# Second block's attention: the first head's rough scores and maxima moved into the projections, the last value tiles into the heads, each head's factor spread behind its scores

## The reference, cut to what matters

```
hn = rms_norm_2(x, norm1_g);  proj = hn @ w_in            # 512 tokens, 1024 -> 18 tiles of 128 features
qa, ka, va, qb, kb, vb = split(proj)                      # A: 8 query heads, 2 key/value heads; B: 8 of each
qa, ka = rope(rms_norm_2(qa)), rope(rms_norm_2(ka))       # norm over the 64 features of a head
out_a = softmax(qa ka^T / 8) va                           # all 512 keys
out_b = mixture over three dilated windows of softmax(rms_norm_2(qb) rms_norm_2(kb)^T / 8 + bias) vb
x = x + concat(rms_norm_2(out_a), rms_norm_2(out_b)) @ w_out
```

## Time and profile before

| | |
|---|---|
| median of 3 runs | 2938.24 us (2937.76 to 2941.49) |
| the profiled execution: time, span | 2937.71 us, 2935.9 us |
| TensorE busy | 2868.0 us (98%), granted clock 0.995 on the mean |
| VectorE, ScalarE, GpSimd busy | 1373.8 us, 1140.3 us, 15.2 us |
| last projection tile's products end | about 2366.1 us from the span's start |
| attention block | 2369.4 to 2513.5 us |

### The profile page before, as it was taken

How to read it: one execution, slowest core, us unless ns; L and a number is a source line. 1 busy time by engine, 2 the same in 40 slices (tenths; PEclk the granted TensorE clock), 3 DMA queues, 4 the chain that set the end, 5 groups by cost and what they waited for, 6 DMA issues and landing times. The chain is left out here.

```text
span 2935.9 us, 41186 instructions
## 1 busy us (share of the span) xinstructions
PE 2868.0 (98%) x17312; PEld 2416.9 (82%) x17312; DVE 1373.8 (47%) x1900; ACT 1140.3 (39%) x1633; POOL 15.2 (1%) x28
## 2 busy tenths in 40 slices
PE   7999999999999999999999999999999999999998
PEld 7888888778888888888888878888888878888887
DVE  3334355676333354333346677233354367655641
ACT  3223244544222244232234555222245356444430
POOL 0000000000000000000000000000000000000000
PEclk9999999999999999999999999999999999999999
DMA  4223411103223421223412103223432201222231
GB/s 150 94 101 127 144 35 58 42 3 115 86 100 108 143 101 58 94 93 121 143 37 78 49 3 109 79 93 101 144 103 78 72 27 39 101 66 100 94 129 51
DMA packets 71560, 254.50 MB, mean 87 GB/s; under 512 B 8072, under 2 KB 9224, under 8 KB 71376
## 3 DMA queue, kind: packets, MB, share of 16 engines
q1 hardware_dynamic: 71376, 251.86, 25.5%
HBM read 249.73 MB, written 2.10 MB: 86 GB/s over the span
## 5 line engine op out<-in xcount | busy, mean ns | idle before, releaser
L214 PE MATMUL ps<-h_hi,w_space 128*128 128x512 f32 (+1 forms) x5056 | 1444.5, 369 | 2.9 <-DVE h_lo L312 2.9
L214 PEld LDWEIGHTS ps<-h_hi,w_space 128*128 128x128 f32 x5056 | 918.5, 189 | 164.0 <-DVE h_lo L312 3.6
L202 DVE TENSOR_TENSOR w_space<-w_raw,w_space 128x1024 fp32r<-128x1024 f32 x440 | 533.7, 1224 | 1016.9 <-ACT w_space L195 1016.8
L214 PE MATMUL ps<-h_lo,w_space 128*128 128x512 f32 (+1 forms) x2528 | 929.8, 368 | 0.0
L195 ACT CAST w_space<-w_raw 128x1024 fp32r<-128x1024 f32 x440 | 457.0, 1051 | 899.9 <-PE ps L214 550.2
L224 PE MATMUL ps<-w_space 128*128 128x512 f32 x3216 | 739.9, 391 | 2.3 <-PEq L91 1.4
L224 PEld LDWEIGHTS ps<-w_space 128*128 128x128 f32 x3216 | 604.2, 188 | 127.9 <-issue 1.6
L214 PEld LDWEIGHTS ps<-h_lo,w_space 128*128 128x128 f32 x2528 | 477.5, 189 | 77.5 <-issue 0.5
L589 ACT CAST w_space<-act_p 128x512 fp32r<-128x512 f32 x88 | 54.8, 623 | 186.1 <-DVE act_p L601 186.1
L604 DVE TENSOR_TENSOR w_space<-act_p,w_space 128x512 fp32r<-128x512 f32 x88 | 61.0, 693 | 60.6 <-ACT w_space L589 60.6
L601 DVE TENSOR_TENSOR act_p<-act_s,ps 128x512 f32<-128x512 f32 x88 | 60.0, 682 | 54.9 <-PE ps L214 54.9
(11 more groups left out here) (407 smaller groups left out, 2227.2 us busy)
## 6 DMA issues: line engine op xcount, KB each, us to landing
w_raw<-in_w_ffn_in SPq DMA_DIRECT2D x176, 512.0 KB, 3.5
w_raw<-in_w_ffn_out SPq DMA_DIRECT2D x88, 512.0 KB, 3.6
w_raw<-in_w_in SPq DMA_DIRECT2D x64, 512.0 KB, 3.5
w_raw<-in_w_up SPq DMA_DIRECT2D x44, 512.0 KB, 3.5
w_raw<-in_w_out SPq DMA_DIRECT2D x24, 512.0 KB, 4.1
w_raw<-in_w_down SPq DMA_DIRECT2D x22, 512.0 KB, 3.5
w_raw<-in_w_ple_gate SPq DMA_DIRECT2D x16, 512.0 KB, 3.6
gain_pre<-in_gains_pre SPq DMA_DIRECT2D x10, 512.0 KB, 4.7
```

The lines of the kernel that those rows point to most:

```text
L202: nc.vector.tensor_tensor(self.lo(n), self.raw[:, n % SLOTS, :], self.hi(n).bitcast(F32), ALU.subtract).then_inc(self.lo_ready, 1)
L214: m = nc.tensor.matmul(c.ps[:, bank, t], part[:, cols], moving[:, k, t], start=(k == 0 and i == 0), stop=(k == KD - 1 and i == 2))
```

## The change

- Behind tile 16 TensorE also makes the first head's four rough scores, in banks 2, 3, 6 and 7, and turns two value tiles (banks 5 and 4) instead of one; behind tile 17 and at the end no value tile is turned, only the maxima.
- VectorE takes those four maxima and negates them behind tile 16, and writes the rows of maxima behind tile 17. ScalarE makes `first_k_hi` for head 0 behind tile 14, runs one Exp on one column behind the roots of tile 16, and copies two value tiles there; its copies at the end go.
- GpSimd writes the ones rows of `first_k_hi`. One of two subtractions for `first_q` goes.
- Attention starts with head 0's scores; head 1's rough scores are dealt among them, the exponents of head 0 come ahead of the second head's operands.
- In heads 0 to 7 the spread comes behind the scores. Value tiles 3 and 4 (of five) are turned at the end of heads 2 and 4 (bank 7), and ScalarE copies them there behind that head's exponents.

```diff
+def write_top_rows(nc, c, rows, bank):      # as top_rows before
+def values_to_tokens(nc, c, bank, tile):    # four transposes, as values_back before
+def copy_token_values(nc, c, bank, j):      # as copy_values before
...
-    SUM_BANK, SPREAD_BANKS, VALUE_BANKS = 4, (2, 3), (5, 2, 3, 6, 7)
+    SUM_BANK, SPREAD_BANKS, VALUE_BANKS = 4, (2, 3), (5, 5, 4)
+    ROUGH_BANKS, TOP_BANK = (2, 3, 6, 7), 7
...
     def tensor_after(self, pe, nc, n):
...
-        if n >= 16:
-            if n == 16:
-                pe.wait_ge(self.normed, self.NA)
-            self.values_back(pe, nc, n - 15)
+        if n == 16:
+            pe.wait_ge(self.normed, self.NA)
+            pe.wait_ge(self.first_lo, 2)
+            for i, bank in enumerate(self.ROUGH_BANKS):
+                nc.tensor.matmul(c.ps[:, bank, :], c.first_q[:, 0, i * P:(i + 1) * P], c.first_k[:, :], start=True,
+                                 stop=True).then_inc(self.rough, 1)
+            pe.wait_ge(self.v_copied, 1)
+            self.values_back(pe, nc, 1)
+            pe.wait_ge(self.rooted, 2)
+            self.values_back(pe, nc, 2)
 
     def tensor_end(self, pe, nc):
-        self.values_back(pe, nc, 3)
-        self.values_back(pe, nc, 4)
+        pe.wait_ge(self.tops_low, 1)
+        nc.tensor.transpose(self.c.ps[0:NT, self.TOP_BANK, S - P:S], self.neg_top[:, :],
+                            self.c.mat["ident"]).then_inc(self.tops_turned, 1)
...
         if n == 16:
             self.roots(act, nc, self.NA, len(self.TILES))
-        if n == 17:
+            nc.scalar.activation(self.unread[:, :], c.eps[:, 0:1], ACT.Exp)
             self.copy_values(act, nc, 1)
-
-    def scalar_end(self, act, nc):
-        for j in range(2, 5):
-            self.copy_values(act, nc, j)
+            self.copy_values(act, nc, 2)
...
+            self.first_tops(dve, nc)
+        if n == 17:
+            self.first_top_rows(dve, nc)
...
+                def late_values(h):
+                    pe.wait_ge(b_normed, h + 1)
+                    values_to_tokens(nc, c, 7, B_V + LATE_VALUES[h] - 1).then_inc(late_turned, 1)
-                for i in range(NT):
-                    rough_scores(0, i)
-                turn_tops(0)
+                scores(0, 0)
+                scores(0, 1)
+                scores(0, 2)
+                rough_scores(1, 0)
+                rough_scores(1, 1)
+                scores(0, 3)
+                rough_scores(1, 2)
+                rough_scores(1, 3)
                 for h in range(TOTAL):
+                    for i in range(NT):
+                        if 0 < h and h + 1 < TOTAL:
+                            rough_scores(h + 1, i)
+                        if h:
+                            scores(h, i)
                     if h < HEADS:
...
+                        if h - 1 in LATE_VALUES:
+                            pe.wait_ge(late_copied, h // 2)
                         pe.wait_ge(widened, h + 1)
                         spread_head_factors(nc, c, 7, wide, len(NORM_A) + h).then_inc(spread, 1)
-                    for i in range(NT):
-                        if h + 1 < TOTAL:
-                            rough_scores(h + 1, i)
-                        scores(h, i)
...
+                    if h in LATE_VALUES:
+                        late_values(h)
...
-                nc.scalar.copy(k_hi[0][0:DH, :], c.proj[k_rows, k, :]).then_inc(firsts, 1)
                 first_parts(1)
+                for j in range(NT - 1):
+                    exponent(0, j)
                 widen(0)
+                exponent(0, NT - 1)
+                widen(1)
+                first_parts(2)
                 nc.scalar.copy(ident_r[:, :], c.mat["ident"]).then_inc(consts, 1)
-                for h in range(TOTAL):
+                for h in range(1, TOTAL):
...
+                    if h in LATE_VALUES:
+                        act.wait_ge(late_turned, h // 2)
+                        copy_token_values(nc, c, 7, LATE_VALUES[h]).then_inc(late_copied, 1)
...
-                for i in range(NT):
-                    maximum(0, i)
-                lowered(0)
                 rests(1)
-                top_rows(0)
```

More of the change, by code:

```diff
@@ L2254, in spread_head_factors @@
     return m
+def write_top_rows(nc, c, rows, bank):
+    return nc.vector.tensor_tensor(rows.rearrange("p (n q) -> p n q", n=NT),
+                                   c.ps[0:NT, bank, S - P:S].unsqueeze(1).to_broadcast([NT, NT, P]),
+                                   c.mats[0:NT, MATS.index("ident"), 0:NT].unsqueeze(2).to_broadcast([NT, NT, P]), ALU.mult)
+def values_to_tokens(nc, c, bank, tile):
+    for n in range(NT):
+        m = nc.tensor.transpose(c.ps[:, bank, n * P:(n + 1) * P], c.proj[:, tile, n * P:(n + 1) * P], c.mat["ident"])
+    return m
+def copy_token_values(nc, c, bank, j):
+    return nc.scalar.copy(c.v_tok[:, :, 2 * j:2 * j + 2, 0:DH],
+                          c.ps[:, bank, :].rearrange("p (n h d) -> p n h d", n=NT, h=2))
 class HeadNorm:
-    SUM_BANK, SPREAD_BANKS, VALUE_BANKS = 4, (2, 3), (5, 2, 3, 6, 7)
+    SUM_BANK, SPREAD_BANKS, VALUE_BANKS = 4, (2, 3), (5, 5, 4)
+    ROUGH_BANKS, TOP_BANK = (2, 3, 6, 7), 7
     TILES, NA = NORM_A + NORM_B, len(NORM_A)
@@ L2269, in __init__ @@
         self.wide = st.sb("wide", [P, 2, NT, 2, DH])
+        self.top, self.neg_top, self.unread = st.sb("top", [P, NT]), st.sb("neg_top", [P, NT]), st.sb("unread", [P, 1])
+        self.first_lo, self.rough, self.tops_found = st.sem("first_lo"), st.sem("rough"), st.sem("tops_found")
+        self.tops_low, self.tops_turned = st.sem("tops_low"), st.sem("tops_turned")
         self.squared, self.summed, self.rooted = st.sem("squared"), st.sem("summed"), st.sem("rooted")
@@ L2287, in gpsimd @@
         pool.wait_ge(self.ones_set, 1)
+        nc.gpsimd.memset(c.first_k_hi[TOP_ROWS, :].bitcast(F32), 1.0).then_inc(self.ones_set, 1)
+        pool.wait_ge(self.ones_set, 2)
     def sums(self, pe, nc, i, count):
@@ L2300, in values_back @@
         self.wait_tile(pe, tile)
[L2301 to L2304, removed]
+        values_to_tokens(nc, c, self.VALUE_BANKS[j], tile).then_inc(self.v_turned, 1)
     def tensor_after(self, pe, nc, n):
@@ L2348, in copy_values @@
         act.wait_ge(self.v_turned, j + 1)
-        nc.scalar.copy(c.v_tok[:, :, 2 * j:2 * j + 2, 0:DH],
-                       c.ps[:, self.VALUE_BANKS[j], :].rearrange("p (n h d) -> p n h d", n=NT, h=2)).then_inc(self.v_copied, 1)
+        copy_token_values(nc, c, self.VALUE_BANKS[j], j).then_inc(self.v_copied, 1)
     def scalar_after(self, act, nc, n):
@@ L2389, in first_head_hi @@
         nc.scalar.copy(c.first_k[k_rows, :], c.proj[k_rows, k, :]).then_inc(self.first_hi, 1)
+        nc.scalar.copy(c.first_k_hi[0:DH, :], c.proj[k_rows, k, :])
     def first_head_lo(self, dve, nc):
@@ L2394, in first_head_lo, with first_tops, first_top_rows @@
         dve.wait_ge(self.first_hi, 3)
[L2395 to L2398, removed]
+        nc.vector.tensor_tensor(c.first_k[other, :], c.proj[k_rows, k, :], c.first_k[k_rows, :].bitcast(F32),
+                                ALU.subtract).then_inc(self.first_lo, 1)
+        nc.vector.tensor_tensor(c.first_q[0:DH, 1, :], c.proj[q_rows, q, :], c.first_q[q_rows, 0, :].bitcast(F32),
+                                ALU.subtract).then_inc(self.first_lo, 1)
+    def first_tops(self, dve, nc):
+        c = self.c
+        for i, bank in enumerate(self.ROUGH_BANKS):
+            dve.wait_ge(self.rough, i + 1)
+            nc.vector.tensor_reduce(self.top[:, i:i + 1], c.ps[:, bank, :], AX, ALU.max).then_inc(self.tops_found, 1)
+        dve.wait_ge(self.tops_found, NT)
+        nc.vector.tensor_scalar(self.neg_top[:, :], self.top[:, :], -1.0, None, ALU.mult).then_inc(self.tops_low, 1)
+    def first_top_rows(self, dve, nc):
+        dve.wait_ge(self.tops_turned, 1)
+        write_top_rows(nc, self.c, self.c.first_q[TOP_ROWS, 1, :], self.TOP_BANK)
     def norm(self, dve, nc, t):
@@ L2512, in full_attention_stage @@
         widened, spread, b_normed = st.sem("widened"), st.sem("spread"), st.sem("b_normed")
+        late_turned, late_copied = st.sem("late_turned"), st.sem("late_copied")
+        LATE_VALUES = {2: 3, 4: 4}
         q_hi, q_rest, k_both = (st.sb(n, [P, 3, S], F32R) for n in ("q_hi", "q_rest", "k_both"))
@@ L2556, in rough_scores @@
                 def rough_scores(h, i):
-                    u, keys = NT * h + i, keys_of(operands_of(h)[4])
-                    if i == 0 and h:
+                    u, keys = NT * (h - 1) + i, keys_of(operands_of(h)[4])
+                    if i == 0 and h == 1:
+                        pe.wait_ge(firsts, firsts_by(h))
+                    elif i == 0:
                         pe.wait_ge(operands, operands_by(h))
@@ L2583, in scores @@
                         nc.tensor.matmul(o, ident_r[:, :], bias_of(bias_lo, h, j), start=False, stop=False)
-                    if j == 0:
-                        pe.wait_ge(tops_ready, h + 1)
-                        if h == 0:
```

(29 more changed lines are left out.)

18 lines of the change are left out of this document (8 added, 10 removed).

## The result

The changed kernel took 2944.76 us (median of 20 runs, 2937.57 to 2948.71), the kernel before 2937.93 us (20 runs, 2936.73 to 2941.84). The ratio is 1.0020 with a 95% interval of 1.0014 to 1.0026: slower by 6.8 us, outside my range. Two of the twenty took 2937.6 and 2937.7, eighteen 2940.4 to 2948.7.

The account below looks back on a forecast made before the run. TensorE, busy 98% of the span, bounds the kernel, so only its idle or low-clock time counts. Terms: -1.4 at the high clock, +1.3 and +1.7 for low clock, +1.6 on 2937.71, so 2939.3 us; range 2935.4 to 2942.2.

Parts of the forecast that it names:

- Start-up of attention: End of projections through head 0: moving head 0's first work behind tile 16 brings the marker 4.45 us earlier.
- The marker: Second product of head 1's first scores, ending the start-up: forecast at 2376.6 against 2381.04 before, -4.45 us.
- The repeated table load: Rival at attention's start: Exp table loaded again, head 0's chain 1.28 us longer, time 2940.6 us; chance 0.14.
- Stalls of heads 3 to 6: TensorE waiting for exponents at the fourth scores tile: +1.66 us for heads 3 and 5, -0.05 head 4, +0.39 head 6.
- Sum at the high clock: Start-up, work still owed, stalls and moved spreads added without any low clock: -1.4 us.
- The clock, first place (head 0, +1.3): TensorE nearly idle from 2374.5 to 2376.6, so a low stretch falls on heads 1 and 2: +1.3 us.
- The clock, second place (head 6): Head 6's two gaps become one of 2.9 us, with a low stretch of 3.4 us behind it: +1.7 us.
- a stretch longer than 3.4 us at both places: Slower rival behind head 0 and head 6: low clock lasts two stretches at both, 2942.7 us; chance 0.06.

## Why the prediction was wrong, point by point

- **Start-up of attention:** right. The marker came 4.77 us earlier, predicted 4.45. The repeated table load did not come: the exponents start at 2369.18, right behind the casts, and the load of 1.28 stands behind tile 16. The Trainium skill (ScalarE activation tables: per-element evaluation and per-set limits, Table sets in the compiler and the runtime) says that the compiler's back end places the loads per block. The trace bears out no repeat at the start of a block of the program, which is how I read it: the set loaded ahead of the barrier at 2359.43 served behind it at 2369.18.
- **Stalls of heads 3 to 6:** right in kind and nearly in size: 0.89, 0.75, 0.76 and 2.63 us, predicted about 0.9, 1.0, 0.9 and 2.9.
- **Sum at the high clock:** sign right, a little rosy. I had 1.4 us of gain left when head 6's values start; 0.65 was there. The heads with a stall took 0.2 to 0.4 us more each than my pitches, as a wait costs more than the idle time of its row: 8.43 us from rough scores to rough scores in head 3 (2388.75 to 2397.18) against 3.27 + 0.47 + 0.36 + 3.57 + 0.36 = 8.03 by my terms.
- **The clock, first place (head 0, +1.3):** right in kind, in one profile of three. Two have no low stretch there; the third has one of 6.8 us over head 1, which costs 2.5 us. The mean is 0.8. The 6.8 low us of before lie ahead of the marker and are in its start-up.
- **The clock, second place (head 6): the step that failed.** That the clock falls behind this gap was right; the term was mis-sized. I priced the low stretch at 3.4 us long, +1.7, with an upper bound of 6.8 long, +3.4, because the longest such stretch that I knew from the trace of before was 6.8, and gave a longer one 0.06, as behind both new gaps TensorE has solid work. Solid in busy time it is, and yet the clock stayed at 1.2 GHz for 10.2, 10.2 and 13.5 us in three profiles, through the value matmuls of 65 columns and for about 5 us of the 512-column products behind them: +5.1 to +6.8. With their mean, 5.7, and 0.8 for head 0, the sum is -0.65 + 5.7 + 0.8 = +5.9 us. Measured in the three profiles, the part from tile 16 to the end of attention takes 5.5 us more than before on the mean, and the medians of twenty executions differ by 6.8. Three profiles and one of before can't tell the rest from the scatter of the low stretches.
- The gap itself I had found, and called it longer than the one at the barrier. What I did not ask is what stood behind each of the gaps whose low stretch I took the price from. Behind the end of attention it was 512-column matmuls at once, in a row that the earlier trace rows doesn't show, and the clock rose 3.6 us into them (the row stands below this list). Whether that difference in the work makes the difference in length is not shown.
- **The range** ended at 2942.2, with slower by over 0.2% at 0.05. My upper bound for a low stretch was the longest that one profile had shown, and that is no bound. One chance of 0.06 was all that I gave to a stretch longer than 3.4 us at both places.

```profile
2513.68 18.16 PE L224 MATMUL ps<-w_space 128*128 128x512 f32 x72 [1.41 <-PEq L91]
```

## What to carry to other kernels

Two short waits with work between them are not the same as one long wait: moving a small, movable operation out of a wait leaves the chain behind the wait where it was and makes TensorE's idle time contiguous. Here waits of 0.7 and 1.3 us left the clock at 2.4 GHz, and one of 2.6 us was followed by 10.2 to 13.5 us at 1.2 GHz. Before such a gap is made, take the price of its low stretch from a gap with like work behind it, and where there is none, leave the upper bound open. Then either keep something running in the gap or take it away at its source. Here that was a copy that waited for TensorE's last work and held an engine's queue: put it behind the first operation that the other engine needs next.

## What the runs showed that I had not expected

- A low stretch of 10.2 us during which TensorE is 100% busy in the rows. The clock was still low behind 4.9 us of value matmuls of 65 columns (1.90 us for sixteen at the high clock, 3.51 at the low one), and came back 5.3 us into the 512-column products that followed.
- Work that nobody reads made the program faster: ten matmuls in the gap by 5.5 us. Fourteen behind it add 3.4 us of work, and the median did not rise (2942.48 against 2944.40).
- A wait costs more than the idle time of its row: moving the late copies takes away 1.65 us of waits and 2.1 us of time.
